# Splitting an expert gather by slot halves, with one expert between the parts, in a two-layer encoder kernel

## The reference

```python
g_logits = t @ w_group + b_group;  g_idx = argmax(g_logits);  g_w = max(softmax(g_logits))
e_sel = expert logits of the group g_idx;  top_v, top_i = top_k(e_sel, 2)
gates = g_onehot * (g_w * softmax(top_v) at top_i)          # (256, 4, 4): two experts of 16 for each token
for each of the 16 experts:
    out += (silu(t @ w_gate) * (t @ w_up) * gates) @ w_down # w_gate, w_up (1024, 512), w_down (512, 1024)
```

## Time and profile before

| what | value |
|---|---|
| median of 3 runs | 727.9 us |
| the profiled execution | 727.73 us, of which the span is 725.9 us |
| mean granted clock of TensorE | 0.994 of full speed |
| TensorE busy | 706.7 us (97%) |
| DVE, ACT, POOL busy | 301.5, 166.1, 26.4 us |
| DMA | 250.87 MB, 346 GB/s on average |
| expert phase of layer 0 | about 147 to 355 us |
| expert phase of layer 1 | about 480 to 689 us |

### The profile page before, as it was taken

The page is one execution under the profiler, slowest core; times in us unless marked ns, Lnnn a source line. Parts: engine busy times, 40 slices in busy tenths (PEclk is TensorE's granted clock), DMA queues, the critical chain, the costliest instruction groups (busy, mean ns, idle before and its releaser), DMA issues.

```text
span 725.9 us, 8170 instructions
## 1 busy us (share of the span) xinstructions
PE 706.7 (97%) x3062; PEld 328.4 (45%) x3062; DVE 301.5 (42%) x717; ACT 166.1 (23%) x395; POOL 26.4 (4%) x47
## 2 busy tenths in 40 slices
PE   9999999999999999989999999999999999989996
PEld 5488454564333333333445545455333333333344
DVE  1213361545437343433322557263535534324324
ACT  3000241432111111110331144252111111112132
POOL 0500000000000000000000000000000000000000
PEclk9999999999999999999999999999999999999999
DMA  9998448889999999999999851489999999999941
GB/s 344 376 285 293 184 174 328 331 310 367 421 409 424 424 431 424 426 418 422 398 381 409 328 197 79 180 284 355 412 412 426 429 422 424 428 420 422 406 164 59
DMA packets 46056, 250.87 MB, mean 346 GB/s; under 512 B 4200, under 2 KB 5448, under 8 KB 25536
## 3 DMA queue, kind: packets, MB, share of 16 engines
q1 hardware_dynamic: 43648, 245.04, 84.4%
q0 software_dynamic: 2048, 5.07, 2.2%
q10 hardware_dynamic: 320, 0.22, 0.1%
HBM read 247.15 MB, written 4.73 MB: 347 GB/s over the span
## 4 chain that ended last, share of the span: by engine, by line
PE 81%; DMA 9%; SPq 5%; issue 2%; DVE 2%; ACT 1%; POOLq 0%; POOL 0%; ACTq 0%; DVEq 0%
PE bank L1024 25%; PE bank L699 24%; PE bank L1041 12%; SPq L454 4%; DMA weights<-in_moe_w_up_dram 4%; PE bank L732 4%; DMA weights<-in_moe_w_down_dram 4%; PE bank L1049 3%; PE bank L983 2%; PE bank L926 2%; PE bank L684 1%; PE bank L1033 1%; DMA weights<-in_even_w_in_dram 1%; PE bank L712 1%; PE bank L770 0%
## 5 line engine op out<-in xcount | busy, mean ns | idle before, releaser
L1024 PE MATMUL bank<-weights,expert_rows 128*64 128x512 f32 x992 | 222.5, 600 | 6.2 <-DMA weights<-in_moe_w_up_dram 6.2
L699 PE MATMUL bank<-weights,normalised 128*128 128x512 f32 (+1 forms) x448 | 191.4, 580 | 0.9 <-DVE normalised L1699 0.7
L1024 PEld LDWEIGHTS bank<-weights,expert_rows 128*64 128x64 f32 x992 | 73.7, 138 | 147.1 <-issue 145.8
L699 PEld LDWEIGHTS bank<-weights,normalised 128*128 128x128 f32 x448 | 83.1, 190 | 91.4 <-issue 88.5
L1041 PE MATMUL bank<-weights,hidden_turned_odd 128*64 128x512 f32 x256 | 58.8, 598 | 0.4 <-DMA weights<-in_moe_w_down_dram 0.4
L1041 PE MATMUL bank<-weights,hidden_turned 128*64 128x512 f32 x224 | 51.5, 598 | 1.3 <-DVE hidden_turned L2029 0.6
L1534 ACT ACTIVATE gate_tanh<-bank 128x256 f32<-128x256 f32 x32 | 12.3, 384 | 175.2 <-PE bank L1024 175.2
L1385 ACT ACTIVATE expert_outputs<-bank 64x512 fp32r<-64x512 f32 (+1 forms) x32 | 18.9, 591 | 117.7 <-PE bank L1041 112.3
L2029 DVE COPY hidden_turned<-bank 128x256 f32<-128x256 f32 x16 | 6.8, 424 | 75.0 <-PE bank L1033 75.0
L2060 DVE TENSOR_TENSOR expert_outputs<-bank,expert_outputs 64x512 fp32r<-64x512 f32 x30 | 20.5, 684 | 41.7 <-ACT expert_outputs L1385 41.5
L2029 DVE COPY hidden_turned_odd<-bank 128x256 f32<-128x256 f32 x16 | 6.8, 424 | 63.3 <-PE bank L1033 63.1
(11 more groups left out here) (276 smaller groups left out, 647.1 us busy)
## 6 DMA issues: line engine op xcount, KB each, us to landing
weights<-in_moe_w_down_dram SPq DMA_DIRECT2D x60, 1024.0 KB, 19.6
weights<-in_moe_w_gate_dram SPq DMA_DIRECT2D x32, 1024.0 KB, 8.7
weights<-in_moe_w_up_dram SPq DMA_DIRECT2D x32, 1024.0 KB, 10.1
weights<-in_moe_w_gate_dram SPq DMA_DIRECT2D x16, 2048.0 KB, 16.5
weights<-in_moe_w_up_dram SPq DMA_DIRECT2D x16, 2048.0 KB, 21.0
weights<-in_even_w_in_dram SPq DMA_DIRECT2D x5, 2048.0 KB, 20.4
weights<-in_ple_w_gate_dram SPq DMA_DIRECT2D x4, 2048.0 KB, 31.5
weights<-in_even_w_out_dram SPq DMA_DIRECT2D x2, 2048.0 KB, 32.5
```

The lines of the kernel that those rows point to most:

```text
L699: mm = pe.matmul(B[bank][:, 0:width], XT[:, k, tok(t)], w[:, k, :], start=(k == 0), stop=(k == KD - 1))
L1024: mm = pe.matmul(bank[j * BLK:(j + 1) * BLK, :].rearrange("p (m f) -> p m f", m=2), rows[:, k, :], W[:, slots, a:a + FF // 2], start=(k == ...
```

## The change

It does four things in each layer.

1. The gather is divided by slots, not by k: first all 8 k for slots 0 to 255 (32 products of 256 columns), then all 8 k for slots 256 to 511 (32 more). Two k share a bank. The matrix of ones and zeros is made in two halves too. Evacuations are 256 wide: k = 0, 1, 4, 5 by ACT and 2, 3, 6, 7 by DVE, 16 in all. The eight small evacuations for expert 0 go.
2. TensorE's order becomes: gather of the first slots (with the sums of tile 1 opened in its middle), both halves of expert 0, gather of the other slots, first half of expert 1, spread, second half of expert 1. Expert 0 reads XS.
3. The spread becomes two products of a column or a matrix of ones with 512 columns of diagonals, one in fp32r and one in float32, which DVE makes from the identity.
4. SP issues a 1 MB load for expert 2 (XD) after the last store of the side product, not before it; ACT seeds the sums of tile 1 after its first two evacuations, and DVE builds the table of offsets after the second half of the one-hots. One small DVE instruction (a column of ones in fp32r) joins the prologue.

The diff, cut to its core:

```diff
-def rows_bank(k):
-    return (0, 1, 4, 5, 1, 4, 1, 4)[k]
+def rows_bank(half, k):
+    return ((0, 1, 4, 5), (5, 4, 1, 4))[half][k // 2]
+def in_bank(k):
+    return slice(256 * (k % 2), 256 * (k % 2) + 256)
+def by_act(k):
+    return k in (0, 1, 4, 5)
+def evac_count(half, k):
+    return 4 * half + 2 * (k // 4) + k % 2 + 1
...
# SP
                         side_half_stored(0)
-                        sp.wait_ge(sem("side_ready"), 4 * l + 4)
+                        sp.wait_ge(sem("side_copied"), 4 * l + 4)
+                        side_half_stored(1)
                         sp.dma_start(XD[:, :], srcs[2][l * NE + 2][0:256, :].rearrange("(p c) d -> p (c d)", c=2))\
                             .then_inc(sem("down2_landed"), 16)
-                        sp.wait_ge(sem("side_copied"), 4 * l + 4)
-                        side_half_stored(1)
...
# TensorE
+                def gathered(half, k):
+                    for t in range(TT):
+                        for part in range(2):
+                            mm = pe.matmul(B[rows_bank(half, k)][:, in_bank(k)], HSP[part][:, t, k:D:KD],
+                                           PH[:, t, 256 * half:256 * half + 256], start=(t + part == 0), stop=(t + part == TT))
+                    mm.then_inc(sem("rows_ready"), 1)
+                def gathered_first():
+                    pe.wait_ge(sem("onehots_ready"), 4 * l + 2)
+                    pe.wait_ge(sem("hs_low"), 3 * l + 2)
+                    pe.wait_ge(sem("side_copied"), 4 * l + 2)
                     for k in range(4):
-                        gathered_part(k, t)
+                        gathered(0, k)
+                    pe.wait_ge(sem("side_copied"), 4 * l + 4)
+                    open_sums(1)
                     pe.wait_ge(sem("hs_low"), 3 * l + 3)
+                    for k in range(4, KD):
+                        gathered(0, k)
+                def gathered_second():
+                    pe.wait_ge(sem("onehots_ready"), 4 * l + 4)
+                    for k in range(KD):
+                        if k == 0:
+                            pe.wait_ge(sem("rows_by_dve"), 8 * l + evac_count(0, 7))
+                        elif k == 2:
+                            pe.wait_ge(sem("rows_by_act"), 8 * l + evac_count(0, 5))
+                        elif k == 6:
+                            pe.wait_ge(sem("rows_by_dve"), 8 * l + evac_count(1, 3))
+                        gathered(1, k)
                 def spread():
-                    pe.wait_ge(sem("gates_ready"), l + 1)
-                    pe.wait_ge(sem("rows_by_act"), 4 * (l + 1))
-                    pe.wait_ge(sem("rows_by_dve"), 4 * (l + 1))
-                    for c in range(4):
-                        pe.matmul(B[4][:, tok(c)], RT[:, 404 + c:405 + c].to_broadcast([P, P]), ident, start=True, stop=True)
-                    for c in range(4):
-                        mm = pe.matmul(B[Y_BANK][:, tok(c)], RT[:, 86 + c:87 + c].to_broadcast([P, P]), ident, start=True, stop=True)
+                    pe.wait_ge(sem("rows_by_act"), 8 * (l + 1))
+                    pe.wait_ge(sem("rows_by_dve"), 8 * (l + 1))
+                    pe.wait_ge(sem("diagonals_ready"), 2 * (l + 1))
+                    pe.matmul(B[4][:, :], ONE[:, 0:1].to_broadcast([P, P]), PT2.rearrange("p n s -> p (n s)"), start=True, stop=True)
+                    mm = pe.matmul(B[Y_BANK][:, :], C[:, C_ONE:C_ONE + P], SPREAD, start=True, stop=True)
                     mm.then_inc(sem("srow_ready"), 1)
...
-                gathered_first(0)
-                pe.wait_ge(sem("side_copied"), 4 * l + 4)
-                open_sums(1)
-                gathered_first(1)
-                first_rows(0)
-                first_rows(1)
-                for k in range(4, KD):
-                    for t in range(TT):
-                        gathered(k, t)
-                other_rows(0)
+                gathered_first()
+                first_expert()
+                gathered_second()
+                second_expert(0)
                 spread()
-                other_rows(1)
+                second_expert(1)
...
# ACT, after the side rows
+                act.wait_ge(sem("side_first_stored"), 16 * (l + 1))
+                rows_evac(0, 0)
+                rows_evac(0, 1)
+                for half in range(2):
+                    seed(1, half)
+                act.wait_ge(sem("onehots_ready"), 4 * l + 4)
+                rows_evac(0, 4)
+                rows_evac(0, 5)
...
+                for part in range(2):
+                    rows_evac(1, 4 * part)
+                    rows_evac(1, 4 * part + 1)
+                    act.wait_ge(sem("rows_by_act"), 8 * l + evac_count(1, 4 * part + 1))
+                    act.wait_ge(sem("rows_by_dve"), 8 * l + evac_count(1, 4 * part + 3))
+                    rows(1, offs, slice(4 * part, 4 * part + 4), ("xe_first", "xe_ready")[part], (1, 2)[part])
...
# DVE
+                gather_onehots(0)
+                rows_low(1, 4, KD)
+                gather_onehots(1)
...
+                rows_evac(0, 2)
                 dve.wait_ge(sem("side_second_stored"), 16 * (l + 1))
-                rows_evac(3)
+                rows_evac(0, 3)
+                rows_evac(0, 6)
+                dve.wait_ge(sem("side_third_stored"), 16 * (l + 1))
+                rows_evac(0, 7)
...
+                for k in (2, 3, 6, 7):
+                    rows_evac(1, k)
+                diagonal = ident.unsqueeze(1).to_broadcast([P, 4, P])
+                for out, a in ((PT2.rearrange("p n s -> p (n s)"), 404), (SPREAD, 86)):
+                    dve.tensor_tensor(out.rearrange("p (c s) -> p c s", c=4), diagonal, RT[:, a:a + 4].unsqueeze(2).to_broadcast([P, 4, P]),
+                                      ALU.mult).then_inc(sem("diagonals_ready"), 1)
```

More of the change, by code:

```diff
@@ L978, in experts @@
                 side_part(1, 1, 1)
-                def gathered_part(k, t):
-                    for part in range(2):
-                        mm = pe.matmul(B[rows_bank(k)][:, :], HSP[part][:, t, k:D:KD], PH[:, t, :], start=(t + part == 0),
-                                       stop=(t + part == TT))
-                    if t == 1:
-                        mm.then_inc(sem("rows_ready"), 1)
-                def gathered_first(t):
-                    pe.wait_ge(sem("onehots_ready"), 2 * l + t + 1)
-                    pe.wait_ge(sem("hs_low"), 3 * l + 1 + t)
+                def gathered(half, k):
[4 more added lines that the diff above has]
+                    mm.then_inc(sem("rows_ready"), 1)
@@ L1170, in experts, with row_in_place, first_expert @@
[L1170 to L1176 removed]
+                def row_in_place(k):
+                    pe.wait_ge(sem("rows_by_act" if by_act(k) else "rows_by_dve"), 8 * l + evac_count(0, max(k, 1)))
+                def first_expert():
+                    wait_unit(u0)
+                    wait_unit(u0 + 1)
+                    gate_up(B[gu_bank(0)], XS[:, :, 0:BLK], pair(u0), lambda: wait_second(u0, u0 + 1), sem("gate_up_halves"),
+                            row_ready=row_in_place).then_inc(sem("gate_up_ready"), 1)
@@ new lines, in second_expert @@
+                def second_expert(half):
+                    n = u0 + 3
+                    if half == 0:
+                        pe.wait_ge(sem("xe_first"), l + 1)
+                        pe.wait_ge(sem("rows_by_act"), 8 * l + evac_count(1, 1))
+                        wait_unit(n)
+                        wait_unit(n + 1)
+                        gate_up(B[gu_bank(1)], XE[:, 1], pair(n), None, sem("gate_up_halves"), (0,))
+                    else:
+                        pe.wait_ge(sem("xe_ready"), NE * l + 2)
+                        gate_up(B[gu_bank(1)], XE[:, 1], pair(n), lambda: wait_second(n, n + 1), None, (1,))\
+                            .then_inc(sem("gate_up_ready"), 1)
@@ L1482, in experts @@
                             seed(0, half)
-                for half in range(2):
-                    seed(1, half)
                 def rows(e, off=None, part=slice(0, KD), done="xe_ready", count=1):
@@ new lines, in experts @@
+                act.wait_ge(sem("side_first_stored"), 16 * (l + 1))
[6 more added lines that the diff above has]
+                rows_evac(0, 5)
+                act.wait_ge(sem("g_below_max"), l + 1)
+                act.activation(RT[:, 20:28], RT[:, 20:28], ACT.Exp).then_inc(sem("g_exp"), 1)
+                act.wait_ge(sem("second_below_first"), l + 1)
@@ L1503, in experts @@
+                act.activation(RT[:, 84:86], RT[:, 84:86], ACT.Exp).then_inc(sem("second_exp"), 1)
                 act.wait_ge(sem("table_ready"), 2 * l + 1)
                 offs = act.value_load(TBL[0:1, 1:2], min_val=0, max_val=LAST)
[L1505 to L1523 removed]
@@ L1970, in experts, with gather_onehots @@
                 dve.wait_ge(sem("iota_ready"), 2 * (l + 1))
-                for t in range(TT):
-                    then(dve.tensor_scalar(TMP[:, t, :], IOTA, S2[:, t, :], None, ALU.is_equal))
```

(13 more changed lines are left out.)

80 lines of the change are left out of this document (11 added, 69 removed).

## The result

The kernel after has a median of 748.31 us over 4 runs (746.66 to 749.04), the kernel before one of 727.91 us over 4 runs (726.28 to 729.18): the ratio is 1.0278, with a 95% interval of 1.0251 to 1.0306. The change makes the kernel 2.8% slower. The forecast was 750.0 us within 736 to 755. The profiled execution took 748.7 us, of which the span is 746.9 us.

A forecast was written before the change was run, and what follows sets the result against it. The prediction took DMA, full at 420 GB/s, to set the end of each expert phase. It added 11.3 us of queue lag in each of two layers: 727.7 + 22.6 = 750.3, called 750 us, range 736 to 755.

The forecast's parts named there:

- The gather's price: Gather on TensorE: each 256-column product costs 0.24 us, spaced by its stationary load, between bounds of 0.11 and 0.245 us.
- Rival (a): Gather: the load costs little at 256 columns (0.11 to 0.14 us a product), total 735 to 739 us; chance 0.14.
- The timetable: Layer 0 on TensorE: gather starts 147.15 us, expert 1's first half read at 174.1, expert 2 at 183.8, 6.3 us later.
- The spread: After expert 1's first half: two products take 1.3 us instead of 1.98, gain 0.7 us, diagonals made under cover.
- The queue: Weight loads on SP: dry some 9 us, four loads at 174.1 us, DMA lag 11.3 us per layer sets the end.
- Rival (b): Expert phases: the queue's lag does not reach the end, TensorE alone decides, 2 x 1.0 us, about 730; chance 0.08.
- Nothing gives it back, because the full stretch is already at 420 GB/s: Rest of each expert phase: DMA cannot make up its lag of 11.3 us.
- 4 x 2.49 = 10.0 us: Queue lag: DMA's full stretch starts on load three instead of seven, four loads of 2.49 us more, 10.0 us per layer.
- 1.3 us of later start: Queue lag: DMA's full stretch starts at 174.1 us instead of 172.8, 1.3 us per layer.
- TensorE's slack: Layer 0's expert phase: TensorE has about 5.3 us spare; its 6.3 us lag alone would cost 1.0 us per layer.
- Rival (d): Late in each expert phase: more weight stalls leave the clock low during the last products, up to 758 us; chance 0.08.
- Rival (c): Faster: gathers under 0.14 us on TensorE and DMA making up its dry time, 725 us; chance 0.05.

The follow-up runs named there:

- e2: Kernel after, with rows_split stored k by k so the gather's stationary operand has neighbours, ACT and DVE writing it with a stride: 736.82 us, ratio 1.0137.
- e6: Kernel before with the changed spread alone, two diagonals by DVE and two products in place of 16: 727.21 us, ratio 0.9996.
- e1: Kernel after, with SP issuing the loads that need only expert 0 ahead of those that need expert 1: 740.84 us, ratio 1.0208.
- e3: Kernel after with both edits, neighbours in the gather's stationary operand and SP's order following expert 0: 729.31 us, ratio 1.0029.
- e4: Kernel before with one more product behind each gather product, same strided stationary operand against 256 columns of zeros: 741.84 us, ratio 1.0204.
- e8: Kernel before without expert 7's gate and up weights loaded in either layer (64 of 4096 columns are): 720.83 us, ratio 0.9908.
- e7: Kernel after without expert 7's gate and up weights loaded in either layer (64 of 4096 columns are): 733.42 us, ratio 1.0083.
- e5: Kernel before with only the layout of rows_split changed, so the gather's stationary operand is read without a stride: 730.64 us, ratio 1.0044.
- e11: e3 with DVE's write of the low part of rows_split moved behind the ranking of its token tile: 729.32 us, ratio 1.0018.
- e9: e3 with ACT and DVE going through rows_split in address order, reading with a 32-byte stride and writing neighbours: 730.27 us, ratio 1.0037.

## Why the prediction was right, and where its terms were off

**The gather's price** was 0.24 us, measured 0.247. e2 shows the reason that I had only inferred, the stride: 0.137 us for neighbours. Rival (a), the load at its columns' price, is refuted for this stride. The rule cited with it (the Trainium skill, TensorE: Matmul & The Clock Gate, LDWEIGHTS) does not hold for this strided fp32r operand: the load is recorded with 337 ns and the products start 0.247 us apart, and not 107 ns. Even with neighbours a load is recorded with 192 ns, and the spacing was 0.137 us at 256 columns. For a price of 0.14 us the prediction had 739 us; e2 has that price, in the same order, and took 736.8.

**The timetable** held within 0.5 us: gather 147.49 (forecast 147.15), expert 1's first half read at 174.52 (174.1), expert 2 at 184.19 (183.8). Of the difference 0.41 us was there already ahead of the gather: the router's product L921 starts at 139.89 us, L906 before at 139.48. The evacuations stayed hidden, and so did the diagonals (0.68 us each, from 171.84 us, under expert 1's first half).

**The spread** was 1.3 us, measured 1.28 (174.52 to 175.80); its gain alone is nothing that can be told (e6).

**The queue** was the term that decides, and it held in kind: dry from 165.5 to 174.6 us, four loads at once, then a full stretch to 362.13 us, where the last half of the down weights arrives (forecast 362.6). Rival (b), TensorE alone, is refuted by e1, where TensorE's timetable stays and 6.7 us go, and by layer 0 of e2, where TensorE reaches expert 2 earlier than before and the mark is 2.6 us later. The queue's size was overstated. The rule was "lag = how much later the full stretch has begun, plus 2.49 us for each load still owed". For layer 0 of each kernel, with the number of the load at which the full stretch begins, and the bytes moved from there to the last landing (to 351.3, 351.0, 358.5, 359.2, 362.1 and 353.9 us) with their mean rate beside it:

| kernel | full from | lag by the rule | shift of the mark | MB to the last landing, GB/s |
|---|---|---|---|---|
| before | 7th load, 172.76 us | 0 | 0 | 75.0, 420 |
| e3 | 7th, 172.35 | -0.4 | -0.3 | 75.2, 421 |
| e1 | 7th, 179.78 | 7.0 | 7.1 | 75.2, 421 |
| e4 | 7th, 179.79 | 7.0 | 7.9 | 75.2, 419 |
| after | 3rd, 174.63 | 11.8 | 10.8 | 78.6, 419 |
| e2 | 3rd, 167.44 | 4.6 | 2.6 | 78.3, 420 |

```profile
174.60:362.10 187.50, 179.25 (x803) 65.73 (x803) 82.08 (x170) 33.66 (x62) 0.00 (x0) 0.99 1.00 419
```
```profile
167.40:353.90 186.50, 177.83 (x803) 65.58 (x803) 82.48 (x170) 33.69 (x62) 0.00 (x0) 1.00 1.00 420
```

(The windows of the kernel after and of e2; that of the kernel before is in the earlier trace rows.) The rule is good to 0.9 us where the kernel starts its full stretch at the same load as before, and 1 to 2 us too high where four loads stand ready at once. Each row is one profiled execution. "Nothing gives it back, because the full stretch is already at 420 GB/s" held: the mean rate is the same. What was mis-sized is the term "4 x 2.49 = 10.0 us" of owed loads. Four loads are 4.2 MB, and the kernel after had only 78.6 - 75.0 = 3.6 MB more to move than the kernel before, which is 8.6 us at 419 GB/s. The sum took the kernel before to owe nothing of its fifth and sixth loads when its seventh goes out. But they were issued from 167.20 us on, and from there to 172.80 us DMA moved 301 GB/s, 1.7 MB with all other traffic, so at least 0.4 of their 2.1 MB were still to come. The other term, 1.3 us of later start, measured 1.9 us, so the two errors partly cancel: 11.3 us per layer became 10.8 and 10.2, and the sum 750.3 became 748.3.

**TensorE's slack** was put at 5.3 us a layer, from the waits of 3.2 and 0.42 us and 1.7 us of lowered clock, and that was nearly right. By its marks (350.81 and 680.57 us) e8 gains 3.5 and 3.4 us in the two layers, and 1.42 and 1.58 us of waits for weights are left in them: together 4.9 us a layer. In e7 the marks (357.30 and 693.29 us) are 3.0 and 2.9 us a layer later than in the kernel before, with 1.5 us of such waits in each. So TensorE by itself would be some 1.5 us late per layer, where I had 1.0, and case (b) some 731 us, where I had 730: estimates, since no run is without the waits.

**Rival (d)**, a clock that stays low to the end, did not come: the granted clock from 185 to 362 us was 0.99, and only expert 13 was long again (8.78 us, as in the kernel before with 8.71). Expert 12 had waited 2.74 us as well and took 7.09 us.

**Rival (c)**, faster, needed gathers under 0.14 us. e3 has them (0.137 us), and the right order of loads too, and is at 1.0029 and not below 1: the cheaper load is paid for by the writes of `rows_split` (e5).

**The sum of the parts.** Of 20.4 us, the order of SP's loads holds 6.7 to 7.5 and the gather's load price 10.7 to 11.5. The 2.1 us that are left with both mended stand ahead of layer 1's gather (e3), and e5 and e11 say that they come from the mend rather than from the change.

## What to carry to other kernels

Measure whether a product costs by its columns or by the load of its stationary operand before dividing it: here, with a strided operand, 256 and 512 columns cost the same, and dividing each product in two doubled the price of the gather. When an order of work moves, go through every queue that issues in a fixed order and ask which ready entries now stand behind an entry that became late; an engine that is never idle later cannot give such a hole back. And where a layout is changed to make one reader cheap, look at what its writer pays, and whether that writer is on a chain that someone waits for; here it ate what the reader had left to win. Last, when a run removes a cause, look at what is left of it before you call the gain its whole size (e8).

## What the runs showed of the hardware that was not expected

- ACT and DVE pay for a stride on either side: 128 x 1024 elements took 1160 ns (ACT) and 1284 ns (DVE) with neighbours on both sides, 2068 and 2044 ns with writes 512 bytes apart, 2157 and 2099 ns with reads 32 bytes apart (e3, e9).
- The fp32r gather has a spacing of 0.242 to 0.247 us at 256 and at 512 columns with a strided stationary operand, and 0.137 us at 256 columns with neighbours (e2, e4).
- The mean rate of DMA over a full stretch was 419 to 421 GB/s in all six kernels of the table, whether four loads stood ready at its start or two. Over 190 to 230 us alone it was 427 and 426 GB/s behind four ready loads and 410 to 426 behind pairs (410 in e4, 426 in e9), so such a short window does not tell the two apart.
